# Third block of a hybrid decoder trunk: two value units and six value tiles ahead of the last four query tiles

## What is computed

```
qp, fp, ip, gp = split(h @ w_in)                   # 4 x 1024 columns, 8 heads of 128
f = lower_bound + (1 - lower_bound) * sigmoid(fp)
q = silu(qp);  k = 1 - f;  log_f = log(f);  v = ip
A = cumsum(log_f)                                  # along the tokens
o[t] = sum_{s<=t} (q[t] . exp(A[t] - A[s]) k[s]) v[s]  +  (q[t] exp(A[t])) @ S
S_new = exp(A_end) * S + (k exp(A_end - A))^T v
out = (head_norm(o) * silu(gp)) @ w_out
```

## Time and profile before

| | |
|---|---|
| three timed runs | 1516.8, 1517.97, 1511.55 us (median 1516.8) |
| the profiled execution, time | 1510.73 us |
| its span in the trace | 1508.9 us |
| busy: PE, DVE, ACT, POOL | 98%, 77%, 62%, 6% of the span |
| mean granted TensorE clock | 0.994 |

### The profile page before, as it was taken

The page is one execution under the profiler, slowest core; times in us unless marked ns, Lnnn a source line. Parts: engine busy times, 40 slices in busy tenths (PEclk is TensorE's granted clock), DMA queues, the critical chain, the costliest instruction groups (busy, mean ns, idle before and its releaser), DMA issues.

```text
span 1508.9 us, 23251 instructions
## 1 busy us (share of the span) xinstructions
PE 1479.9 (98%) x8573; PEld 1312.6 (87%) x8573; DVE 1157.2 (77%) x1306; ACT 936.5 (62%) x975; POOL 88.3 (6%) x96
## 2 busy tenths in 40 slices
PE   9999999999999989999999999999999999999997
PEld 8899888999999979989788888888888888888885
DVE  5756677555455697777798888988889888898897
ACT  5434555334333774354777877778777787777875
POOL 1023110000000000120300000000000000000011
PEclk9999999999999999999999999999999999999999
DMA  8577724997445523451999999999999999999994
GB/s 250 134 136 139 138 88 135 284 296 208 123 145 175 159 84 114 144 159 60 362 406 381 389 362 394 378 377 385 363 393 380 377 389 358 391 379 379 395 334 170
DMA packets 213588, 404.03 MB, mean 268 GB/s; under 512 B 13471, under 2 KB 130491, under 8 KB 213390
## 3 DMA queue, kind: packets, MB, share of 16 engines
q1 hardware_dynamic: 202976, 372.82, 71.0%
q0 software_dynamic: 6320, 22.20, 4.9%
q10 hardware_dynamic: 4222, 8.05, 1.4%
HBM read 372.74 MB, written 30.28 MB: 267 GB/s over the span
## 4 chain that ended last, share of the span: by engine, by line
PE 87%; DVE 6%; ACT 3%; DMA 2%; issue 1%; POOL 0%; SPq 0%; DVEq 0%; ACTq 0%; POOLq 0%
PE bank L509 26%; PE bank L510 25%; PE bank L511 25%; PE bank L733 1%; DVE dense_lo L1878 1%; PE bank L1151 1%; DMA arena<-in_w_moe_down 1%; PE bank L775 1%; PE bank L678 1%; DVE w_lo L2361 1%; DVE arena L2007 1%; PE bank L725 1%; ACT dense_hi L1374 0%; PE bank L987 0%; PE bank L1100 0%
## 5 line engine op out<-in xcount | busy, mean ns | idle before, releaser
L2361 DVE TENSOR_TENSOR w_lo<-arena,w_hi 128x2048 fp32r<-128x2048 f32 (+1 forms) x280 | 596.9, 2165 | 87.1 <-ACT w_hi L1716 85.9
L1716 ACT ACTIVATE w_hi<-arena 128x2048 fp32r<-128x2048 f32 (+1 forms) x280 | 501.2, 1819 | 119.7 <-PE bank L511 114.2
L509 PE MATMUL bank<-w_hi,xg_hi 128*128 128x512 f32 (+1 forms) x768 | 287.3, 374 | 0.3
L510 PE MATMUL bank<-w_lo,xg_hi 128*128 128x512 f32 (+1 forms) x768 | 286.1, 373 | 0.0
L511 PE MATMUL bank<-w_hi,xg_lo 128*128 128x512 f32 (+1 forms) x768 | 285.4, 372 | 0.0
L1878 DVE TENSOR_TENSOR dense_lo<-ring,dense_hi 128x2048 fp32r<-128x2048 f32 (+1 forms) x78 | 167.8, 2151 | 122.0 <-ACT dense_hi L1374 121.9
L1374 ACT ACTIVATE dense_hi<-ring 128x2048 fp32r<-128x2048 f32 (+1 forms) x78 | 140.5, 1802 | 139.9 <-PE bank L511 114.7
L509 PEld LDWEIGHTS bank<-w_hi,xg_hi 128*128 128x128 f32 x768 | 144.5, 188 | 29.0 <-issue 3.1
L511 PEld LDWEIGHTS bank<-w_hi,xg_lo 128*128 128x128 f32 x768 | 144.2, 188 | 25.8
L510 PEld LDWEIGHTS bank<-w_lo,xg_hi 128*128 128x128 f32 x768 | 144.5, 188 | 24.9
L509 PE MATMUL bank<-h_hi,dense_hi 128*128 128x320 f32 x448 | 143.3, 320 | 3.9 <-DVE h_lo_a L1891 1.4
(11 more groups left out here) (458 smaller groups left out, 2383.2 us busy)
## 6 DMA issues: line engine op xcount, KB each, us to landing
arena<-in_w_moe_down SPq DMA_DIRECT2D x176, 512.0 KB, 6.7
arena<-in_w_moe_gate SPq DMA_DIRECT2D x128, 512.0 KB, 7.0
arena<-in_w_moe_up SPq DMA_DIRECT2D x128, 512.0 KB, 7.2
arena<-in_w_moe_gate SPq DMA_DIRECT2D x64, 384.0 KB, 5.7
arena<-in_w_moe_up SPq DMA_DIRECT2D x64, 384.0 KB, 4.1
ring<-in_w_in_ab SPq DMA_DIRECT2D x32, 512.0 KB, 9.2
ring<-in_w_in_c SPq DMA_DIRECT2D x32, 512.0 KB, 4.7
expert_rows<-ZERO SPq DMA_DIRECT2D x12, 1024.0 KB, 7.7
```

What stands on the lines that cost most here:

```text
L509: mm(out, left[0], right[0], start=start, stop=False)
L510: mm(out, left[0], right[1], start=False, stop=False)
L1716: fn(WH[SLOT_OF[p]][:, 0:unit_size(p)], STAGE[:, s, 0:unit_size(p)], ACT.Copy).then_inc(S("unit_hi"), 1)
L2361: v.tensor_tensor(WL[w][:, 0:n], STAGE[:, s, 0:n], WH[w][:, 0:n].bitcast(F32), ALU.subtract).then_inc(S("unit_split"), 1)
```

## The change

The steps v0 to v5 and q4 to q7 change places in `C_STEPS`, with the steps that go with them, and the units in `C_ORDER` likewise: both units of column group 4 (v0 to v5) are loaded and split ahead of both of group 1 (q4 to q7). Between the level steps la4 and la7 stand v0 to v3 in place of q4 to q7. v4, v5 and then q4 to q7 follow, with la8 and turn0 between them. `silu1` moves behind q7 with them, and so stands behind `xend0` and ahead of `xb0`; `xb0`, `pb0`, `db1` and `xb1` stand behind q7 too, `out0` comes between lb0 and lb1, v6 behind the second `wl`. The number of steps of each kind and all arithmetic stay.

```diff
-    q4 sig1 pa5 forget4 la5 q5 forget5 xa6 la6 wh forget6 forget7 pa6 ln1 da7 scan1 xa7 q6 q7 wl la7 pa7 silu1 end0
-    xend0 kend0 v0 xb0 v1 pb0 wh db1 wh xb1 wl lb0 turn0 lb1 v2 la8 v3 db2 pb1 v4 wl wh xb2 wl out0 v5 v6 pb2
+    v0 sig1 pa5 forget4 la5 v1 forget5 xa6 la6 wh forget6 forget7 pa6 v2 ln1 da7 scan1 xa7 v3 wl la7 pa7 end0
+    xend0 kend0 v4 wh v5 q4 la8 q5 turn0 wl wh q6 q7 silu1 xb0 pb0 db1 xb1 wl lb0 out0 lb1 db2 pb1 wh xb2 wl v6 pb2
@@
-        C_ORDER = [2, 0, 3, 1, 4, 5, 6, 7]
+        C_ORDER = [2, 0, 3, 4, 1, 5, 6, 7]
```

## The result

| | before | after |
|---|---|---|
| runs taken side by side, median | 1512.12 us (7 runs, 1507.48 to 1517.97) | 1524.15 us (7 runs, 1520.87 to 1529.94) |
| ratio of the times | | 1.0073, 95% interval 1.0047 to 1.0098 |
| profiled execution, time | 1510.73 us | 1523.53 us |
| its span | 1508.9 us | 1521.7 us |
| mean granted TensorE clock | 0.994 | 0.991 |

The changed kernel is slower: 12.0 us between the medians, 12.8 us between the two profiled spans. (The ratio is not the quotient of the two medians, which is 1.0080 and lies inside its interval.) The forecast was 1526 us with a loss of 11.5 us.

A forecast was written before the change was run, and what follows sets the result against it. PE (TensorE), busy 98% of the span, was taken as the bound. A loss of 9.8 us up to lb2 plus 1.7 of slow clock made 11.5, on a mean of 1514.3: 1526 us, range 1516 to 1533.

The forecast's parts named there:

- What bounds: PE is full from 719 us to the end, so a microsecond lost earlier comes back one for one.
- Part 1: Tiles exchanged between level steps: la5 still starts at 546.65, its wait 0.7 us longer; la6 starts at 552.2, not 552.6.
- Part 2: ACT's split after la6 waits for v2, the logarithm queued behind; DVE's scan1 starts at 564.1 instead of 559.08, 5.0 late.
- Part 3: What hangs on scan1: PE waits 2.3 us ahead of q4 and 2.4 to 4 us ahead of q6.
- Part 4: Second group's chain from silu1 loses cover: lb0 waits 1.8, v6 2.1; lb2 starts at 604.9, not 595.03; loss 9.8 us.
- The clock: Slow clock behind PE's waits: one low stretch of 1.7 us taken, with bounds of 0 and 5.1 us.
- third rival: Waits ahead of lb0, v6 and lb2 let the clock fall twice or three times: 13.2 to 15 us; 20%.
- The rule weighed: About 1.38 us of drain per ACT table switch, for ln1 and xb0: 2.8 us more, 14.3 in all; kept out.
- The gain said to be possible at most: PE's waits ahead of la5, la6 and v0, plus 1.7 us of slow clock: 6.4 us at most.

The follow-up runs named there:

- e6: Changed kernel with eight matmuls of zeros added on PE ahead of q6, in its wait; 1522.20 us, 1.0072 of the kernel before.
- e1: Changed kernel with v2's copy and ACT's split, its wait included, moved behind the logarithm; 1520.74 us, 1.0065 of the kernel before.
- e5: Kernel before with one wait added on ACT: ahead of forget6 until PE has finished q6; 1515.60 us, 1.0028 of the kernel before.
- e2: Changed kernel with xb0, db1, xb1 and the split of v6's unit ahead of q6 and q7, out0 ahead of lb0; 1516.76 us, 1.0048 of before.
- e4: Kernel before with only DVE's split of v0's unit moved ahead of scan1 from behind q7; 1511.51 us, 1.0003 of the kernel before.
- e7: Kernel before with five matmuls of zeros added on PE ahead of v0, in its wait; 1510.12 us, 0.9984 of the kernel before.
- e8: Changed kernel with the edits of e1 and e2, and the splits of v3 to v5's and q6's units moved; 1509.07 us, 0.9985 of before.
- e9: e8 with v0 to v2 one level step earlier, ACT's wh ahead of forget7 and DVE's wl ahead of scan1; 1505.91 us, 0.9968 of before.

## Why the prediction was right, point by point

The prediction's times are on the scale of the kernel before; since the block began 1.3 us earlier, 1.3 us is to be added to those of the changed kernel before they are set beside them.

**What bounds.** It said that a microsecond lost before 719 us comes back one for one, as PE is full to the end. The rest of the run took 789.4 us before and 788.5 after, so it did. Inside the block one thing did take up a delay: the wait of 1.23 us for the state's load at 678.04, which the kernel before has and the changed one has not.

**Part 1.** la5 was to wait 1.8 us and la6 to start at 552.2. The waits are 0.84 and 1.53, and la6 starts at 552.84 on that scale. The low clock of 0.61 over 541 to 544, in la4 and v0, stood in no term. It isn't free: la5 and the scan come 0.65 us later from the entry than in e6 (60.78 for 60.14, 78.07 for 77.42), which has the same order up to there and the clock at 1.00.

**Part 2** held in every step. ACT's split was put at 557.1 behind 2 us of waiting: it is at 556.31 (557.6 on that scale) behind 2.07. The scan was put 5.0 us late: it is 5.5 late from the entry, 4.8 in e6. e1 and e5 show the cause from both sides, by taking the wait together with the split and a copy off the logarithm's way in the new order (lb2 5.1 sooner, some 3.5 of it by the edit), and by putting a wait of 3.8 us into the old (4.2 later). No run takes the wait alone out of the new order.

**Part 3.** Waits of 2.3 ahead of q4 and of 2.4 to 4 ahead of q6 were forecast; they are 2.53 and 3.89. The splits that end them were put at 569.6 and 583.1; they end at 568.9 and 582.1 (570.1 and 583.4 on that scale).

**Part 4** held for lb0 (1.93 for 1.8), and the chain from `silu1` to lb2 takes 13.06 us where its times add up to 12.9. e2 gives it a price of 5.3 us. PE's side of it was wrong for **v6**, which was to wait 2.1 us: its row has no wait in it. lb0, out0 and lb1 ran at the 1.2 GHz level for 3.4 us, and so PE came to v6 just as its split ended (601.86, v6 at 601.91). What stands as 2.1 us of waiting in the sum was mostly 1.7 us of slow matmuls. That changed nothing in the result, because the split and what DVE does behind it set v6's and lb2's start either way.

**The clock** was the mis-sized term. It had one low stretch of 1.7 us, the size of the old one. Two stretches cost time up to lb2: 2.5 us in q6 and q7, and 0.65 by way of la4 and v0. The one from lb0 to lb1 is free, as said. Together that is 3.2 us for 1.7, and it is nearly all of what lb2 is later than forecast (13.1 for 11.5). PE's busy time is 4.0 us longer up to lb2, where the sum had a net of nothing (one stretch in, one out), and its idle time 9.1 us, where the sum had 9.8 + 1.7 = 11.5; the two together are again 13.1 for 11.5.

**The time, and luck in it.** The block lost 15.0 us, not 11.5. Behind lb2, where nothing was to be added or given back, a late low stretch took 3.0 us and the missing wait for the state's load gave 1.2 back. The spans are only 12.8 us apart because this execution came to the block 1.3 us sooner and was 0.9 us shorter behind it, which no step of the prediction provides for. A loss of 15 us in the block is what the third rival (more low clock) had as its upper end. The forecast of 1526 us lies close to the median of 1524.15, but it starts from 1514.3 for the kernel before, whose median beside the changed kernel was 1512.12; the loss between the medians, 12.0 us for 11.5, is the fairer comparison.

**The rule weighed.** It asked for two more drains of 1.38 us, for 14.3 us in all. In the changed kernel the logarithm's table load starts at 560.70, takes 1.28, and the logarithm starts at 561.99; the exponential's starts at 593.80 and its first instruction at 595.10. Those are gaps of 0.01 and 0.02 us. The Trainium skill (ScalarE: Activation LUTs, What ACT_TABLE_LOAD costs) adds a drain to each switch; behind the load neither row shows one, and ahead of it ACT goes on within 0.02 us as well (`silu1` ends at 593.78). The measurement decides: a switch costs its 1.28 us here.

**The gain said to be possible at most.** I gave 6.4 us as what idle time and low clock could return. e4 and e7 show that the 2.39 + 1.7 us ahead of and in v0 could not be had by themselves: with either gone, DVE's chain from scan1 over the weighed keys to group b's products is late next, and lb2 moves by +0.7 and -0.6 us. A gain takes a schedule that puts DVE's work into DVE's own waits and gives PE tiles meanwhile, as e8 does (3.0 us).

**What stays open.** The late low stretch is in the profiled executions of the changed kernel and of e1 to e4 and e6 to e9, though shorter in some, and not in those of before and e5. What brings it on was not found. The order of tiles doesn't decide it: e4 has the list of the kernel before but for one split, some 100 us earlier, and has the stretch (0.54 over 661 to 670). The idle time of before and e5 nearby (1.23 and 1.67 us, for the state's load) doesn't either, as it lies some 11 us behind the place. Each kernel has one profiled execution, so how often each has the stretch isn't known. Nor was each piece of e2's edit (silu1 against the exponentials, the split and the products) tried alone.

## What to carry to other kernels

When steps are reordered in a list that several in-order engines walk, look first for waits that the move newly creates on an engine other than the one that is to gain: here ACT's split came to depend on the tile just moved behind it, and a logarithm that feeds DVE stood behind it in ACT's queue. DVE's chain came 5 us later, though ACT's row shows a wait of only 2: the rest of the delay was filled with other work and doesn't look like waiting. Compare when an instruction starts, not only how long it waits. Moving one producer (here q6 and q7 with their SiLU) later also moves the whole chain that starts at it away from the work that covered it, so move the chain's independent part the other way. And count an idle stretch ahead of a tile as winnable only as far as the engine that releases it has slack of its own up to the next thing that PE needs from it.

## What the runs showed of the hardware

- The same wait at the same place was followed by a fall of the clock in one execution and by none in another. la4 waits 1.59 us in the kernel before and in e4, whose lists are the same up to there; the clock is then 1.00 over 539 to 545 in the first and 0.72 in the second. The changed kernel (0.61 over 541 to 544) and e8 (1.00 from 541 to 600) differ in the same way. The row of before, then that of e4:

```profile
540.88 1.16 PE L987 MATMUL bank<-arena 128*128 128x128 f32 x8 [1.59 <-DVE arena L2243]
```

```profile
539.23 1.75 PE L987 MATMUL bank<-arena 128*128 128x128 f32 x8 [1.59 <-DVE arena L2243]
```

- The clock fell with PE busy throughout: 0.57 over 672 to 680 in the changed kernel, in 8.00 us of busy PE. There a matmul whose weights have 8 columns takes 741 ns at most, where its usual time is 433:

```profile
L657 PE MATMUL bank<-arena,cst x32: 432/433/741, 178.6 to 696.5; 128*8 128x320 f32 x32
```
